# Overflow tables cut into parts behind the first expert gates, two low-part splits moved to GpSimd, and the order of four transfers changed, in an attention and mixture-of-experts layer on one core

## The chip, the cores and the metric

One core of one Trainium2 chip runs the whole program. Its engines run side by side and meet at semaphores: TensorE (PE, its weight loads PEld), VectorE (DVE), ScalarE (ACT), GpSimd (POOL), SyncE (SP, which here only issues transfers); 16 DMA engines carry the transfers. The metric is the device time of one execution, in microseconds (us), as the median of several runs.

## What is computed

The reference is one transformer layer on 1024 tokens of width 1024 in fp32: three kinds of attention, an output projection, and a hierarchical mixture of experts; then a last norm. The change lies in the experts, which compute

```python
for e in range(N_EXPERTS):                       # 32 experts, width 256
    a = hf @ w_e_gate[e]
    u = hf @ w_e_up[e]
    out = out + (jax.nn.silu(a) * u * gate[:, e:e + 1]) @ w_e_down[e]
```

where `gate` is zero for all but the two experts that the router chose for a token (top 2 of the 8 experts of the token's best group).

## The kernel before, in words

Each engine has its own program, written out by hand, and the order within a program is fixed. Attention, the output projection and the router (the norm, the logits, the choice of experts) come first. The experts are done as 34 tiles n = 0 to 33 of up to CAP = 96 tokens: one tile for each of the 32 experts and two for tokens that did not fit in their expert's 96 rows (overflow tiles, at n = 16 and n = 25). `TILE[n]` says which expert a tile belongs to.

One expert tile takes these steps. GpSimd gathers 96 token rows from the DRAM tensor `h2_d` into XG (`gather`, L916 before). TensorE transposes them (`x_transposes`, L2247, 8 products), ScalarE copies one half of the result to XT and VectorE the other (`m_x`), and TensorE multiplies with the gate and up matrices (`up_product`, L2256, 128 products). VectorE and ScalarE form the gated activation (`m_gate` on VectorE, `m_exp` on ScalarE) and cut it into a high part aTh and a low part aTl. The down matrix wdn is cut likewise: ScalarE writes the high part wdh (`m_split_hi`), VectorE the low part wdl (`m_split_lo`, L1802, two halves of 128x1024). TensorE multiplies them (`down_product`, L2266, 12 products), ScalarE and VectorE scale one half each into YO (`m_out`), and GpSimd adds the rows into `x2_d` (`scatter`, L928). On TensorE the order is up(n), transposes(n + 1), down(n - 1), up(n + 1) and so on.

The weights of a tile are 2 MB (wgu) and 1 MB (wdn). They go into a ring of RING = 6 slots; SyncE issues all of these transfers, in the order of its program, and one that waits holds up all behind it. The load of tile n (n >= 6) waits until down(n - 6) is done (the semaphore m_dn). The load of tile 5 goes where the overflow tables lie, so it waits for the last operation that uses them, `wrow_ov`.

The overflow tables are made by VectorE from the counts of the router (`overflow_tables`: in_tile, in_row, cj, ej, info), TensorE turns them into lists of token numbers (`overflow_ids` on TensorE, L2238, 16 products), and VectorE reads these (`overflow_ids` on VectorE: ids_ov, wo_hi, wrow_ov). Between the router and the first expert VectorE also works through a chain of small operations (s1 to s16, exc, eb, ge, geb, rae, rs, p1, sl, r, shf, shi, slo), all behind the count `v`; they end in shi and slo, from which only the overflow tables are made. `w_hi` and `wrow` are the weights of the tokens, first read when the output of tile 0 is scaled.

GpSimd's first gather waits for the token numbers `ids` of VectorE and for the stores of all token rows into `h2_d` (`h2_store`, semaphores h_st).

## Time and profile before

| | |
|---|---|
| median of 3 runs | 1179.07 us (1176.46 to 1182.43) |
| profiled execution, its own time | 1181.38 us |
| its span in the trace | 1179.6 us |
| TensorE busy | 1081.4 us, 92% |
| VectorE busy | 681.8 us, 58% |
| ScalarE busy | 448.4 us, 38% |
| GpSimd busy | 254.3 us, 22% |
| granted TensorE clock, mean | 0.972 of full speed |
| moved by DMA | 239.17 MB, mean 203 GB/s |

All times of one execution are counted from the start of its span. The 34 expert tiles take the stretch from about 811 us to 1151 us; what comes before is attention, projection and router, what comes after is the last norm. A share of busy time is an average over all of it and does not say what a stage waits for.

### The profile page before, as it was taken

The page shows a single profiled execution, that of the slowest core. Times are in us where ns is not written, and L with a number is a line of the kernel's source. Part 1 is how long each engine was busy: PE and PEld are TensorE (multiplying, and loading weights), DVE is VectorE, ACT ScalarE, POOL GpSimd, SP SyncE. Part 2 cuts the span into 40 slices and gives each one's busy share as a digit, 9 for nine tenths or more (in the row PEclk, how much of TensorE's full clock was granted, in tenths as well). Part 3 has the DMA queues.
Part 4 walks back from the last instruction along what each step waited for, and adds up shares of the span by engine and source line. Part 5 has one row for each costly group of instructions (what it writes and reads, how often), then busy time and mean ns, then how long its engine had stood idle before and what let it go on. Part 6 is the DMA issues. An engine that isn't in the chain of part 4 may idle for free.

```text
span 1179.6 us, 30191 instructions
## 1 busy us (share of the span) xinstructions
PE 1081.4 (92%) x12242; PEld 920.6 (78%) x12242; DVE 681.8 (58%) x1724; ACT 448.4 (38%) x761; POOL 254.3 (22%) x476
## 2 busy tenths in 40 slices
PE   5999899999999999999999899995989999989990
PEld 5989788778788888888877678885878887878770
DVE  4340445324666766665677533468767676767664
ACT  6321112221455555554576522221333343334323
POOL 1030000000332333321166300001223322222220
PEclk9999899999999999999999999995999999999995
DMA  9020855253656855565332255438899999999948
GB/s 362 21 89 2 291 178 161 107 161 141 156 120 149 207 148 119 120 140 131 107 83 57 104 214 202 138 119 315 309 370 366 362 354 350 344 360 356 354 142 298
DMA packets 62024, 239.17 MB, mean 203 GB/s; under 512 B 23328, under 2 KB 24128, under 8 KB 52032
## 3 DMA queue, kind: packets, MB, share of 16 engines
q1 hardware_dynamic: 54272, 220.45, 55.9%
q0 software_dynamic: 7616, 16.80, 6.1%
q8 instruction: 99, 1.62, 0.6%
q14 instruction: 37, 0.30, 0.1%
HBM read 201.14 MB, written 45.88 MB: 209 GB/s over the span
## 4 chain that ended last, share of the span: by engine, by line
PE 80%; DMA 6%; DVE 5%; issue 4%; ACT 2%; POOL 1%; SPq 1%; POOLq 0%; DVEq 0%; ACTq 0%
PE PS L2256 16%; PE PS L1920 13%; PE PS L2098 9%; PE PS L2266 8%; PE PS L2180 7%; PE PS L1909 6%; PE PS L2076 4%; PE PS L2037 4%; PE PS L2077 3%; PE PS L2247 2%; DMA wst<-in_wt 1%; DMA k<-T_d 1%; PE PS L1955 1%; PE PS L2070 1%; DMA h_d<-h 1%
## 5 line engine op out<-in xcount | busy, mean ns | idle before, releaser
L2256 PEld LDWEIGHTS PS<-XT,wgu 128*64 128x64 f32 x4352 | 185.8, 139 | 32.9 <-issue 32.9
L2256 PE MATMUL PS<-XT,wgu 128*64 128x96 f32 x4352 | 194.2, 250 | 18.0 <-issue 18.0
L1129 ACT ACTIVATE pt<-PS,cst 128x512 f32<-128x512 f32 (+3 forms) x288 | 167.2, 650 | 107.8 <-PE PS L2077 83.9
L1448 DVE CUSTOM_DVE_ANT_0 junkm<-PS,cst 128x512 f32<-128x512 f32 (+3 forms) x276 | 133.5, 531 | 78.4 <-PE PS L2037 76.3
L2098 PEld LDWEIGHTS PS<-V,pt 128*64 128x64 f32 x3840 | 121.6, 138 | 23.2 <-issue 12.0
L2098 PE MATMUL PS<-V,pt 128*64 128x65 f32 x3840 | 137.3, 225 | 0.9 <-issue 0.9
L1920 PE MATMUL PS<-hTh,wth 128*128 128x512 f32 x256 | 103.1, 403 | 5.1 <-DVE wtl L1295 5.1
L1920 PE MATMUL PS<-hTl,wth 128*128 128x512 f32 x256 | 100.7, 394 | 0.0
L1920 PE MATMUL PS<-hTh,wtl 128*128 128x512 f32 x256 | 100.7, 393 | 0.0
L843 POOL TENSOR_SCALAR_AFFINE_SELECT pt<-pt 128x128 f32<-128x128 f32 x224 | 64.1, 292 | 162.2 <-ACT pt L1129 119.1
L928 POOL DMA_INDIRECT x_d<-YO,ids x34 | 61.1, 1797 | 135.3 <-DVE YO L1811 100.9
L1802 DVE TENSOR_TENSOR wdl<-wdn,wdh 128x1024 fp32r<-128x1024 f32 x68 | 80.3, 1222 | 9.3 <-ACT wdh L970 9.2
L2037 PE MATMUL PS<-k,q 128*128 128x128 f32 (+3 forms) x324 | 79.5, 346 | 2.0 <-DMA k<-T_d 1.7
L2076 PE MATMUL PS<-q,k 128*128 128x512 f32 (+1 forms) x228 | 81.2, 370 | 0.0
L2077 PE MATMUL PS<-q,k 65*128 65x512 f32 (+1 forms) x240 | 76.4, 338 | 0.0
L970 ACT ACTIVATE wdh<-wdn 128x1024 fp32r<-128x1024 f32 x68 | 67.7, 1045 | 0.0
L1027 ACT ACTIVATE thi<-PS,cst 128x512 fp32r<-128x512 f32 x32 | 21.8, 686 | 113.7 <-PE PS L1920 92.3
L2037 PEld LDWEIGHTS PS<-k,q 128*128 128x128 f32 (+1 forms) x324 | 56.2, 190 | 10.6 <-DMA k<-T_d 2.5
L1193 ACT ACTIVATE ge<-ge 128x192 f32<-128x192 f32 x34 | 12.4, 364 | 136.8 <-DVE ge L1787 136.8
L1920 PEld LDWEIGHTS PS<-hTh,wth 128*128 128x128 f32 x256 | 48.7, 190 | 16.5 <-DVE wtl L1295 5.6
L916 POOL DMA_INDIRECT XG<-h_d,ids x34 | 33.7, 991 | 128.7 <-PE PS L2247 115.3
L1920 PEld LDWEIGHTS PS<-hTl,wth 128*128 128x128 f32 x256 | 48.8, 191 | 10.9 <-issue 1.0
(288 smaller groups left out, 1887.7 us busy)
## 6 DMA issues: line engine op xcount, KB each, us to landing
wgu<-in_wgu SPq DMA_DIRECT2D x34, 2048.0 KB, 17.6
wdn<-in_wdn SPq DMA_DIRECT2D x34, 1024.0 KB, 23.5
q<-T_d SPq DMA_DIRECT2D x58, 256.0 KB, 4.3
k<-T_d SPq DMA_DIRECT2D x58, 256.0 KB, 5.5
wst<-in_wt SPq DMA_DIRECT2D x16, 512.0 KB, 6.4
T_d<-thi SPq DMA_DIRECT2D x16, 512.0 KB, 2.6
T_d<-tlo SPq DMA_DIRECT2D x16, 512.0 KB, 3.9
xt<-in_x SPq DMA_DIRECT2D x8, 512.0 KB, 12.0
```

The costliest lines, as they stand in the source:

```text
L1129: ins = nc.scalar.activation(pt[:, (n + 2) % 6, 0:nt * P], PS[:, n % 3, 0:nt * P], ACT.Exp, scale=C("slopes", h, h + 1), bias=C("kb", w, w ...
L1448: V_.tensor_tensor_reduce(out=junk_[:, 0:L], in0=PS[:, bank, 0:L], in1=tab, scale=1.0, scalar=-3e38, op0=ALU.add, op1=ALU.max, accum_out=m ...
L1802: V_.tensor_tensor(out=wdl[n % RING][:, c, :], in0=wdn[n % RING][:, c, :], in1=wdh[n % 2][:, c, :].bitcast(f32), op=ALU.subtract).then_inc ...
L1909: ins = mm(o, x[:, k, t * P:(t + 1) * P], wv[w][:, k, :], start=(k == 0 and x is hTh and w == 0), stop=(k == KC - 1 and w == 1))
L1920: ins = mm(PS[:, 2 * p + h, :], w[:, p, k * P:(k + 1) * P], x[:, k, h * 512:(h + 1) * 512], start=(k == 0 and w is wth and x is hTh), stop ...
L2037: ins = mm(PS[:, bank, 0:nk * P], q_[:, t * P:(t + 1) * P], k_[:, k0 * P:(k0 + nk) * P], start=True, stop=True)
L2076: mm(o, k1[:, j * P:(j + 1) * P], q1[:, q], start=True, stop=False)
L2077: ins = mm(o, k2[0:HD + 1, j * P:(j + 1) * P], q2[0:HD + 1, q], start=False, stop=True)
L2098: ins = mm(PS[h * HD:(h + 1) * HD, O_BANK[b % 2], (t % 4) * VW:(t % 4 + 1) * VW], pt[0:rows, (n + 2) % 6, q * P + h * HD:q * P + (h + 1) * ...
L2180: ins = mm(PS[:, 2 + h, :], x[:, t % 2, k, :], w[:, k, h * 512:(h + 1) * 512], start=(k == 0 and x is oth and w is woh), stop=(k == KC - 1 ...
L2256: ins = mm(PS[h * HD:(h + 1) * HD, 2 + p, f * CAP:(f + 1) * CAP], wgu[q][:, c, lo:lo + HD], XT[:, p, c, :], start=(c == 0 and f == 0), sto ...
L2266: ins = mm(PS[0:CAP, 5 + h, :], x[:, p, c, :], w[:, c, cols], start=(c == 0 and x is aTh and w is wdh[p]), stop=(c == 1 and w is wdl[q]))
```

## The change

Lines marked - are taken out, lines marked + are put in; in between, only what the text speaks of is shown.

```diff
         # SyncE
                 if t + 1 == NT:
                     sp_.wait_ge(g_mm, 2 * NT)
-                    load_expert(TILE[2], 2)
+                    sp_.dma_start(wgu[2][:], a["wgu"][TILE[2]].rearrange("p (k n) -> p k n", k=KC)).then_inc(we_in[2], 16)
                 h2_store(t, p)
 
+            sp_.dma_start(wdn[2][:], a["wdn"][TILE[2]].rearrange("p (k n) -> p k n", k=2)).then_inc(we_in[2], 16)
             sp_.dma_start(wdn[3][:], a["wdn"][TILE[3]].rearrange("p (k n) -> p k n", k=2)).then_inc(we_in[3], 16)
...
             load_expert(TILE[4], 4)
+            sp_.wait_ge(m_dn, 1)
+            load_expert(TILE[RING], 0)
             sp_.wait_ge(dve_did, DV.of("wrow_ov"))
             load_expert(TILE[5], 5)
-            for n in range(RING, NB):
+            for n in range(RING + 1, NB):
         # GpSimd
+            def m_split_lo(n):
+                for c in range(2):
+                    pool.wait_ge(m_whi, 2 * n + c + 1)
+                    nc.gpsimd.tensor_tensor(out=wdl[n % RING][:, c, :], in0=wdn[n % RING][:, c, :],
+                                            in1=wdh[n % 2][:, c, :].bitcast(f32), op=ALU.subtract).then_inc(m_plo, 1)
             for n in range(NB):
                 gather(n)
+                if n in (2, 3):
+                    m_split_lo(n - 2)
         # VectorE
             red("v", vt[:, 0, 16:], cmp7[:], ALU.add)
+            m_x(0)
             src = 0
...
-            m_x(0)
-            overflow_tables()
-            m_split_lo(0)
             for n in range(NB):
                 m_gate(n)
                 if n == 0:
-                    overflow_ids()
+                    overflow_tiles()
                 if n:
                     m_out(n - 1)
-                if n + 1 < NB:
+                if n == 1:
+                    overflow_rows()
+                if n == 2:
+                    overflow_ids()
+                if 1 <= n < NB - 1:
                     m_split_lo(n + 1)
         # TensorE
             for n in range(NB):
                 m_up(n)
-                if n == 0:
-                    overflow_ids()
                 if n + 1 < NB:
                     m_transposes(n + 1)
+                if n == 2:
+                    overflow_ids()
                 if n:
                     m_down(n - 1)
```

`overflow_tables` is cut in two: `overflow_tiles` (the in_tile operations) stands behind the gate of tile 0, `overflow_rows` (in_row, cj, ej, info) behind the gate of tile 1 and the output of tile 0, and the reading of the lists behind the gate of tile 2 and the output of tile 1. The load of tile 5 still waits for `wrow_ov`. In `m_gate` of tile 0 the copy of XT for tile 1 stands ahead of the wait for ScalarE's exponential, no longer behind the reciprocal. The pair `w_hi`, `wrow` stands a few operations sooner. Some buffers lie elsewhere (ge, gd, aTh, aTl, and wdh of the odd tiles), and with it ScalarE's high split of tile 1 waits for the last x2 stores and not for TensorE's overflow product.

VectorE behind the chain of small operations that ends in slo, before (XT the transposed tokens, in_tile a table of tiles, wrow the weights of the tokens, cst the constants):

```order
L1736 SCALAR_TENSOR_TENSOR slo<-shi,slf 128x16 [waits dve_did]
L1740 COPY wrow<-PS 96x32 [waits pe_did,dve_did]
L1609 TENSOR_TENSOR wrow<-wrow,PS 96x32 [waits dve_did]
L1774 COPY XT<-PS 128x384 [waits m_tr,dve_did]
L1609 TENSOR_TENSOR in_tile<-shi,cst 128x8x22
L1609 TENSOR_TENSOR in_tile<-shi,cst 128x8x22 [waits dve_did]
```

And VectorE ahead of that chain now (the first row into vt is the count `v`):

```order
L1629 TENSOR_REDUCE vt<-cmp_153 128x32 [waits dve_did]
L1770 COPY XT<-PS 128x384 [waits m_tr,dve_did]
L1628 TENSOR_TENSOR vt<-vt 128x32
L1628 TENSOR_TENSOR vt<-vt 128x32 [waits dve_did] x4
L1629 TENSOR_REDUCE eb<-cmp_153 128x32 [waits dve_did]
L1628 TENSOR_TENSOR eb<-vt,eb 128x32 [waits dve_did]
```

The copy of tile 0's XT has moved from the end of the chain to its beginning, and the tables are gone from behind it.

VectorE at the end of the gate of tile 1, before (YO is the scaled output, here of tile 0; wdl with its numbers 195 is the low part for slot 2):

```order
L1796 CAST aTh<-gd 128x192 [waits link]
L1797 TENSOR_TENSOR aTl<-gd,aTh 128x192 [waits link]
L1811 TENSOR_SCALAR YO<-PS,wrow 96x512 [waits m_dn]
L1802 TENSOR_TENSOR wdl_195<-wdn_189,wdh_179 128x1024 [waits m_whi] x2
L1787 TENSOR_SCALAR ge<-PS 128x192 [waits m_gu]
```

And at the same place now (in_row, cj and ej are tables of rows and of tile numbers):

```order
L1794 CAST aTh<-gd 128x192 [waits link]
L1795 TENSOR_TENSOR aTl<-gd,aTh 128x192 [waits link]
L1809 TENSOR_SCALAR YO<-PS,wrow 96x512 [waits m_dn]
L1628 TENSOR_TENSOR in_row<-slo,cst 128x768
L1628 TENSOR_TENSOR in_row<-slo,cst 128x768 [waits dve_did]
L1628 TENSOR_TENSOR cj<-vt,cst 128x672 [waits dve_did]
L1629 TENSOR_REDUCE ej<-cj 128x21 [waits dve_did]
L1755 TENSOR_SCALAR ej<-ej 128x21 [waits dve_did]
L1757 TENSOR_SCALAR ej<-vt 128x1 [waits dve_did]
L1759 CAST info<-ej 1x22 [waits dve_did]
L1800 TENSOR_TENSOR wdl_195<-wdn_189,wdh_179 128x1024 [waits m_whi,dve_did]
L1800 TENSOR_TENSOR wdl_195<-wdn_189,wdh_179 128x1024 [waits m_whi]
```

Seven table operations have come in between the output of tile 0 and the low split of tile 2, and so ahead of the gate of tile 2, which is the next row into ge.

SyncE's weight transfers around the last token store, before (the number behind wgu and wdn goes with the slot: 183 and 189 are slot 2, 184 and 190 slot 3, 185 and 191 slot 4, 186 and 192 slot 5, 181 and 187 slot 0):

```order
L704 DMA wgu_183<-in_wgu 128x4096 [waits g_mm]
L705 DMA wdn_189<-in_wdn 128x2048
L718 DMA h_d<-h_142 128x1024 [waits h_xn]
L741 DMA wdn_190<-in_wdn 128x2048
L743 DMA wgu_184<-in_wgu 128x4096 [waits xg_in0]
L704 DMA wgu_185<-in_wgu 128x4096 [waits h_lg]
L705 DMA wdn_191<-in_wdn 128x2048
L704 DMA wgu_186<-in_wgu 128x4096 [waits dve_did]
L705 DMA wdn_192<-in_wdn 128x2048
L704 DMA wgu_181<-in_wgu 128x4096 [waits m_dn]
```

And now:

```order
L739 DMA wgu_183<-in_wgu 128x4096 [waits g_mm]
L719 DMA h_d<-h_142 128x1024 [waits h_xn]
L742 DMA wdn_189<-in_wdn 128x2048
L743 DMA wdn_190<-in_wdn 128x2048
L745 DMA wgu_184<-in_wgu 128x4096 [waits xg_in0]
L705 DMA wgu_185<-in_wgu 128x4096 [waits h_lg]
L706 DMA wdn_191<-in_wdn 128x2048
L705 DMA wgu_181<-in_wgu 128x4096 [waits m_dn]
L706 DMA wdn_187<-in_wdn 128x2048
L705 DMA wgu_186<-in_wgu 128x4096 [waits dve_did]
```

The last token store is one transfer further ahead, and the load of tile 6 (slot 0, behind down(0)) stands ahead of the load of tile 5 (slot 5, behind `wrow_ov`, which is the wait on dve_did).

On GpSimd the two halves of wdl of tile 0 stand between gather(2) and gather(3), those of tile 1 between gather(3) and gather(4); before, nothing but gathers and scatters stood there. On TensorE the 16 products of the overflow lists stand between the transposes of tile 3 and down(1), before between up(0) and the transposes of tile 1.

## Rows read from the trace of the kernel before

**Rows 1.** The page: DMA engines' busy tenths in 40 slices; GpSimd's queue: packets, MB, share.

```profile
DMA  9020855253656855565332255438899999999948
...
q0 software_dynamic: 7616, 16.80, 6.1%
```

**Rows 2.** Windows: length; busy us of PE, PEld, DVE, ACT, POOL; clock, DMA share, GB/s.

```profile
825.00:830.00 5.00, 2.57 (x33) 2.41 (x33) 4.39 (x11) 2.66 (x4) 0.96 (x1) 0.70 0.36 125
...
840.00:900.00 60.00, 57.05 (x950) 49.48 (x948) 42.85 (x68) 21.32 (x31) 19.22 (x13) 1.00 1.01 359
...
1135.00:1140.00 5.00, 5.00 (x98) 4.39 (x98) 4.64 (x9) 2.58 (x3) 1.45 (x1) 1.00 0.05 15
```

**Rows 3.** The chain that ended last: start us, us, what; up(2), up(32), up(33).

```profile
838.11 5.43 PE PS L2256 x128
...
1127.21 5.43 PE PS L2256 x128
...
1136.24 5.45 PE PS L2256 x128
```

**Rows 4.** SyncE's issues of loads 5, 8, 32; behind 8 and 32, their landing.

```profile
829.44 0.33 SPq L704 DMA_DIRECT2D wgu<-in_wgu  x1
...
856.55 0.43 SPq L705 DMA_DIRECT2D wdn<-in_wdn  x1
...
DMA to landing us min/median/max: 16.3/16.3/16.3
...
1088.51 0.43 SPq L705 DMA_DIRECT2D wdn<-in_wdn  x1
...
DMA to landing us min/median/max: 37.8/37.8/37.8
```

**Rows 5.** The chain around the first tiles: start us, us, what.

```profile
794.37 10.32 DMA h_d<-h
...
805.81 5.13 DMA XG<-h_d,ids
...
815.09 7.97 PE PS L2256 x128
...
827.67 6.83 PE PS L2256 x128
```

**Rows 6.** Timeline of the first tiles: start us, us, engine, line, op, tiles.

```profile
802.95 0.19 DVE L1699 TENSOR_SCALAR ids<-PS 96x32 uint32<-96x32 f32 x1 [0.24 <-PE PS L2215]
...
807.47 0.49 DVE L1610 TENSOR_REDUCE vt<-cmp 128x32 f32<-128x320 f32 x1
...
812.95 1.99 ACT L970 ACTIVATE wdh<-wdn 128x1024 fp32r<-128x1024 f32 x2
...
814.43 0.56 DVE L1774 COPY XT<-PS 128x384 f32<-128x384 f32 x1
...
814.91 0.70 DVE L1609 TENSOR_TENSOR in_tile<-shi,cst 128x176 fp32r<-128x176 f32 x2
...
817.91 1.95 DVE L1609 TENSOR_TENSOR in_row<-slo,cst 128x768 fp32r<-128x768 f32 x2
...
822.27 2.36 DVE L1802 TENSOR_TENSOR wdl<-wdn,wdh 128x1024 fp32r<-128x1024 f32 x2
...
834.54 0.36 DVE L1787 TENSOR_SCALAR ge<-PS 128x192 f32<-128x192 f32 x1 [2.73 <-PE PS L2256]
...
838.54 0.36 DVE L1797 TENSOR_TENSOR aTl<-gd,aTh 128x192 fp32r<-128x192 f32 x1
```

**Rows 7.** GpSimd's products of two SBUF tensors, and VectorE beside them.

```profile
59.88 7.32 POOL L805 TENSOR_TENSOR wnl<-wn,wnh 128x3296 fp32r<-128x3296 f32 x1 [33.58 <-ACT wnh L970]
...
60.78 7.50 DVE L1295 TENSOR_TENSOR wtl<-wst,wth 128x1024 fp32r<-128x1024 f32 x1 [9.42 <-ACT wth L970]
...
602.45 1.30 POOL L854 TENSOR_TENSOR wol<-wraw,woh 128x512 fp32r<-128x512 f32 x1
...
602.76 1.02 DVE L1518 TENSOR_SCALAR r<-r,nlam 128x4 f32<-128x4 f32 x1
```

More of the change, by code:

```diff
@@ L354, in program @@
         XT = at("XT", [P, 2, KC, CAP], f32, ZB + 56 * KB)
-        ge = at("ge", [P, 2 * CAP], f32, ZB + 24 * KB)
-        gd = at("gd", [P, 2 * CAP], f32, ZB + 25 * KB)
-        aTh = at("aTh", [P, 2, 2, CAP], f32r, ZB + 26 * KB)
-        aTl = at("aTl", [P, 2, 2, CAP], f32r, ZB + 26 * KB + 1536)
-        wdh = [at(f"wdh{p}", [P, 2, D], f32r, ZE + 24 * KB * p) for p in range(2)]
+        ge = at("ge", [P, 2 * CAP], f32, ZB + 62 * KB)
+        gd = at("gd", [P, 2 * CAP], f32, ZB + 62 * KB + 8 * CAP)
+        aTh = at("aTh", [P, 2, 2, CAP], f32r, ZE + 30 * KB)
+        aTl = at("aTl", [P, 2, 2, CAP], f32r, ZE + 30 * KB + 16 * CAP)
+        wdh = [at(f"wdh{p}", [P, 2, D], f32r, o) for p, o in enumerate((ZE, ZB + 24 * KB))]
         dead = (4 * COL["dist"][0] + 31) // 32 * 32
@@ L490, in program @@
         m_wlo = sem("m_wlo")
+        m_plo = sem("m_plo")
         m_dn = sem("m_dn")
@@ L550, in program @@
                     + [f"s{k}" for k in (1, 2, 4, 8, 16)]
-                    + ["exc", "eb", "ge", "geb", "rae", "rs", "p1", "sl", "r", "shf", "shi", "slo", "w_hi", "wrow",
+                    + ["exc", "eb", "ge", "geb", "rae", "rs", "p1", "w_hi", "wrow", "sl", "r", "shf", "shi", "slo",
                        "in_tile0", "in_tile1", "in_whi0", "in_wlo0", "in_tok0", "in_whi1", "in_wlo1", "in_tok1",
@@ L1208, in m_split_hi @@
                 act.wait_ge(we_in[n % RING], 32 * (n // RING + 1))
-                act.wait_ge(m_dn, n - 1) if n >= 2 else act.wait_ge(pe_did, PEV.of("ido" if n else "wrow"))
+                if n >= 2:
+                    act.wait_ge(m_dn, n - 1)
+                elif n == 1:
+                    for p in range(2):
+                        act.wait_ge(x2_st[p], 16 * NT // 2)
+                    act.wait_ge(h_xg, 2 * NT)
+                else:
+                    act.wait_ge(pe_did, PEV.of("wrow"))
                 for c in range(2):
@@ L1717, in _, with overflow_tiles @@
             red("v", vt[:, 0, 16:], cmp7[:], ALU.add)
[L1718 to L1743 removed]
+            def overflow_tiles():
                 eq = in_tile[:, :, :, 0, :]
@@ L1814, in _ @@
             m_x(0)
-            overflow_tables()
-            m_split_lo(0)
-            dve.wait_ge(h_ss, NT)
-            for p in range(2):
-                dve.wait_ge(x2_st[p], 16 * NT // 2)
+            src = 0
+            for k in (1, 2, 4, 8, 16):
+                tt(f"s{k}", vt[:, 1 - src, 16:], vt[:, src, 16:], vt[:, src, 16 - k:16 + NE - k], ALU.add)
+                src = 1 - src
+            inc = vt[:, src, 16:]
+            red("exc", eb[:], cmp7[:], ALU.add)
+            tt("eb", eb[:], inc, eb[:], ALU.subtract)
+            D_("ge", V_.tensor_scalar(out=rb[:], in0=rank, scalar1=float(CAP), scalar2=None, op0=ALU.is_ge))
+            D_("geb", V_.scalar_tensor_tensor(out=rc[:, 0, :], in0=eb[:], scalar=float(CAP), in1=C("e31"),
+                                              op0=ALU.mult, op1=ALU.add))
+            tt("rae", rb[:], rb[:], rc[:, 0, :].unsqueeze(1).broadcast_to([P, NT, NE]), ALU.mult)
+            tt("rs", ra[:], rank, C("ecap").unsqueeze(1).broadcast_to([P, NT, NE]), ALU.add)
+            tt("p1", ra[:], ra[:], rb[:], ALU.add)
+            dve.wait_ge(pe_did, PEV.of("wrow"))
+            D_("w_hi", V_.tensor_copy(out=wrow[0:CAP, 0:NE], in_=PS[0:CAP, 4, 64:64 + NE]))
+            tt("wrow", wrow[0:CAP, 0:NE], wrow[0:CAP, 0:NE], PS[0:CAP, 4, 64 + NE:64 + 2 * NE], ALU.add)
+            tt("sl", sel[:], ra[:].unsqueeze(1).broadcast_to([P, 2, NT, NE]), onehot[:], ALU.mult)
+            red("r", slf[:], sel[:], ALU.add)
+            D_("shf", V_.tensor_scalar(out=shi[:], in0=slf[:], scalar1=1.0 / CAP, scalar2=ROUND, op0=ALU.mult,
+                                       op1=ALU.add))
+            D_("shi", V_.tensor_scalar(out=shi[:], in0=shi[:], scalar1=-ROUND, scalar2=None, op0=ALU.add))
+            D_("slo", V_.scalar_tensor_tensor(out=slo[:], in0=shi[:], scalar=-float(CAP), in1=slf[:],
+                                              op0=ALU.mult, op1=ALU.add))
             for n in range(NB):
```

34 lines of the change are left out of this document (8 added, 26 removed).

## The prediction

> **What bounds the kernel now.** I read the slices of the page first. The DMA engines are half idle until the experts begin, and from there nearly full to the end of them [rows 1]. The windows of that stage say how full: share 1.01 at 359 GB/s over 840 to 900 us, while the stretch 835 to 1140 ends with a window of share 0.05, that is 0.25 us of work [rows 2]. So the last weights are in at about 1135.3. The chain that ended last runs through TensorE's products all the same: up(2) starts at 838.1, up(32) at 1127.2, up(33) at 1136.2 [rows 3]. The last two lie 9.0 apart, which is one tile on TensorE with no wait; the mean over the 30 tiles between up(2) and up(32) is 289.1 / 30 = 9.6, since TensorE also stands still now and then.
>
> Then the issues of the weight loads and their landings. The second half of load 8 is issued at 856.6 and lands 16.3 later, at 872.9; that of load 32 is issued at 1088.5 and lands 37.8 later, at 1126.3 [rows 4]. So 24 loads took 253.4 us, 10.6 each, against TensorE's 9.6: the queue gets later by one microsecond a tile. It began the stage far ahead and ends it level: load 32 lands 0.9 before up(32) starts, and the last transfer is done about 0.9 before up(33) starts. Before the stage the reader is to see a hole in the transfers, share 0.36 over 825 to 830 [rows 2]. From 829.4, when load 5 is issued [rows 4], they never stop. So two chains end this stage together: TensorE's, and the transfers', whose end moves with every microsecond that the engines idle once they could be loading. I count both.
>
> **The front of TensorE's chain.** The last token store takes 10.32 from 794.37, and the first gather starts at 805.81 [rows 5]. With 1 MB less ahead of it (2.8 us at 359 GB/s) the store lands near 801.9. The wait that then ends last is the one for the token numbers, ready at 803.1 [rows 6], 1.5 before the store's old landing at 804.7. So the gather moves forward by 1.5, and with it the rows of tile 0 (5.13 behind it [rows 5]) and load 3.
>
> VectorE now waits for tile 0's transposes right behind the count `v`, done at 807.96, and copies XT at 811.0 and not at 814.43 [rows 6]. Up(0) starts at 811.7, before 815.1, and is through in 7.97 (the clock is low there in both), at 819.6.
>
> The chain of small operations ran from 808.0 to the copy at 814.4 [rows 6], so 6.4 us. It now stands between this copy and the gate of tile 0: alone it would run from 811.6 to 818.0 and be hidden behind up(0). Here the moved splits come in. GpSimd took 1.30 for 128x512 and 7.32 for 128x3296 [rows 7]; by the line through both, 128x1024 takes 2.4, a tile's two halves 4.8 (VectorE's two took 2.36 [rows 6]). They start when ScalarE's first high half is done (1.0 each [rows 6], from 811.5), so they cover 812.8 to 817.8.
>
> What does VectorE do beside them? Beside the longer of them its subtraction of two SBUF tensors, which otherwise takes 1.2 us, took 7.50 from 60.78 and ended 1.1 behind GpSimd's product of 59.88 to 67.20 [rows 7]. A 128x4 operation from 602.76 took 1.02 and ended level with GpSimd's of 602.45 to 603.75. VectorE stood still until GpSimd was done. This bears on nearly all of the chain: eb, geb, rae, p1, wrow, sl and slo read two tensors of SBUF, and only a few read PSUM. So each half holds VectorE for about 2 of its 2.4 us; one operation slips in between. The chain ends at 821.9 and the gate of tile 0 starts 2.3 late, not on time.
>
> The Trainium skill, page "SBUF — State Buffer", section "SBUF: two separate sides", says the same: the port pair that VectorE and GpSimd share is locked for a whole instruction, against VectorE operations with two SBUF inputs and those in a two-port mode. It speaks against this change, and the two pairs of rows agree with it; by it the sum is the one worked out here, without it rival 1.
>
> From there: the gate's first operation, then XT of tile 1 on both engines at 823.2, and up(1) at 823.3, before 827.67 [rows 5]: 4.4 ahead. Its 6.83 contain a fall of the granted clock (mean 0.70 over 825 to 830 [rows 2]) behind a wait of TensorE of 2.4; I leave 2.8 of wait there, and so keep 6.83: up(1) ends at 830.1. The splits of tile 1 run on GpSimd from 824.3 to 829.3 and hold up the last two operations of gate 0 (aTh, aTl) until 829.7; down(0), which comes behind up(1) and the transposes, does not wait for it.
>
> The tiles part of the tables took 814.91 to 817.9, so 3.0, the rows part 817.91 to 822.2, so 4.3 [rows 6]. A gate takes 3.0 from its first operation to the end of the XT copy, 4.4 to aTl (834.54 to 838.9 [rows 6]). Behind gate 0 the tiles part ends at 832.75, 2.6 after up(1); XT of tile 2 is there at 835.7, and up(2) starts at 835.8, 2.2 ahead of before. Behind gate 1 (837.1) come the output of tile 0 (0.8), the rows part (4.3) and the low split of tile 2 (2.4): gate 2 begins at 844.7, though up(2) ended at 841.2. XT of tile 3 is ready at 847.7, and up(3) starts at 847.8, before 847.1. TensorE's 1.5 for the overflow products lie inside this wait. Then gate 2, the output of tile 1 and the reading of the lists: `wrow_ov` is done at 850.5. From tile 4 on VectorE is on time again. TensorE's chain alone therefore comes out 0.7 late: what the front gains (3.4, then 4.4) the parts and the lock take back.
>
> **The transfers.** Load 5 waits for `wrow_ov`: issue at 850.6, before 829.4 [rows 4], 21 later. Load 6 takes its place, but can't go before down(0) ends at 833.8. Its 3.1 MB need 8.8 at 359 GB/s and about 1 to begin: done at 843.6. Then SyncE waits, with loads 5 and 7 both behind the same wait, and the engines stand idle but for a gather and a scatter until 851.6. Before, load 5 was through by the same reckoning at 839.2 (829.4 + 1 + 8.8), and from there 28 loads ran on without a gap. The same number (5 and 7 to 33) now starts at 851.6: 12.4 later. One gather and one scatter fewer stand in their way: GpSimd's queue moved 16.8 MB [rows 1] in 68 transfers, so 0.5 MB, 1.4 us. So the last landing moves by 11.0, and of this 0.9 was free: up(33) starts 10.1 later. Load 5 itself lands near 861, up(5) wants it at 866; nothing stalls there, the bill comes at the end, when TensorE's waits for weights set in around tile 22. I take 9 of the 10.1, since the lock's overlap (2 us a half) is the softest term and can only be less.
>
> **What costs nothing, and why.** ScalarE's high split of tile 1 waits for stores long done. The wdn part of load 2 lands 1.3 later, some 20 before its use. GpSimd's gather(3) and gather(4) stand behind splits that end 2.7 and 1.7 before their transposes free them; without this cover a gather would be late by the difference. `w_hi` and `wrow` are early in either place.
>
> **Rivals.** (1) The lock bites little: VectorE's small operations get in first, and GpSimd waits. Against it stand the two pairs of [rows 7], for it that they are only two. Then up(1) starts at 821.6, the clock may hold, up(2) starts at 830.8, load 5 is issued at 845.3, the 28 loads start 7.1 later, less 1.4 and 0.9: +5, 1184.
>
> (2) The transfers give way: faster with fuller queues, or the engines' end not tied to the last landing. Then TensorE's chain counts, with the lock: +0.7, 1180. Against it: 359 GB/s at share 1.01 with two loads queued as with four. The Trainium skill, "HBM Reference", section "Specifications (TRN2)", gives about 425 GB/s for a core that streams alone; by it a load with its gather and scatter would take 8.9 and not 10.6, and this rival would hold. The trace disagrees for this mix.
>
> (3) Faster: rivals 1 and 2 at once, in one mechanism, that the stage is TensorE's alone and VectorE's parts fit behind its products. Up(4) then starts 4.5 earlier, up to 6 if the clock does not fall at up(1): 1174. It decides if load 33 lands more than 5 us ahead of its use after a 12 us later start, which 0.9 of slack speaks against.
>
> (4) Worse: the clock falls a second time in the waits ahead of up(2) and up(3) (2.0 and 1.4 long), and `wrow_ov` slips by 1.5 to 5: +11 to +14, 1192.
>
> **The numbers.** The profiled execution took 1181.38 (span 1179.6), 2.3 over the median of 1179.07. The sum is a difference against that span, and I put it on the median: 1179.07 + 9 = 1188. Chances: forecast 0.46, rival 1 0.22, rival 2 0.12, rival 3 0.13, rival 4 0.07. The forecast's own range is 1185 to 1191. The range leaves out rival 3 and most of rival 4: 1178 to 1192. Half a per cent is 5.9 us, about what a measurement of this kernel can tell from no change (its three runs lie 6 apart). Faster: half of rival 3, 0.07. Slower: nine tenths of the forecast (0.41), a third of rival 1 (0.07), all of rival 4: 0.55. The rest, 0.38, within.
>
> **What would show it.** Up(0) near 811.7 and up(1) near 823; VectorE operations of 2 us where 0.2 was the rule, each ending with a GpSimd subtraction; up(3) near 848; load 5 issued near 850 with a hole of some 8 us ahead of it; waits of TensorE for weights from about tile 22 on, and a last landing near 1146. The forecast is wrong if load 5 is issued before 842, or if the last ten tiles still follow each other 9.0 us apart.

## The result, and the profile after

The changed kernel takes 1185.54 us (median of 20 runs, 1180.21 to 1192.85), the kernel before 1180.99 (20 runs, 1176.46 to 1184.1). The ratio is 1.0037, with a 95% interval of 1.0024 to 1.005: 4.5 us slower, which lies inside half a per cent. One execution of each kernel was profiled, 1183.62 after and 1181.38 before, so the two traces show 2.2 of the 4.5 us.

The page after: busy time of the engines, and the DMA engines' busy tenths in 40 slices.

```profile
PE 1081.6 (92%) x12242; PEld 921.3 (78%) x12242; DVE 683.5 (58%) x1720; ACT 448.6 (38%) x761; POOL 264.1 (22%) x480
...
DMA  9020855253655855565332355438699999999958
```

TensorE did the same work. In the row of the transfers three digits moved by one, and one by more: slice 29 fell from 8 to 6 [rows 1]. From there on the slices are as full as before, so what is missed there has to be made up later or comes on top.

The windows, with the columns of [rows 2] (the last three: granted clock, DMA share, GB/s):

```profile
825.00:830.00 5.00, 5.00 (x98) 4.89 (x94) 4.86 (x6) 0.00 (x0) 3.60 (x2) 0.79 0.06 19
830.00:835.00 5.00, 3.82 (x25) 2.66 (x25) 4.33 (x10) 2.02 (x4) 0.97 (x1) 1.00 0.38 89
...
845.00:850.00 5.00, 3.84 (x87) 3.54 (x87) 4.76 (x11) 2.58 (x3) 0.75 (x1) 1.00 0.37 108
...
820.00:855.00 35.00, 30.03 (x463) 26.49 (x462) 31.59 (x58) 10.13 (x16) 12.54 (x8) 0.95 0.65 223
```

There are two holes, one ahead of load 6 and one ahead of load 5. Over 820 to 855 the DMA engines moved 0.223 x 35 = 7.8 MB. The same window of the kernel before reads

```profile
820.00:855.00 35.00, 32.57 (x534) 29.24 (x532) 26.43 (x45) 10.44 (x16) 7.58 (x6) 0.95 0.89 323
```

which is 11.3 MB. The third busy time is VectorE's: 31.6 of 35 us after, 26.4 before, and TensorE (the first) gives up 2.5 us.

The timeline after, which answers to [rows 6] and to SyncE's issues in [rows 4]; in brackets the idle time before a row and its releaser:

```profile
812.35 4.68 POOL L940 TENSOR_TENSOR wdl<-wdn,wdh 128x1024 fp32r<-128x1024 f32 x2
812.83 4.26 DVE L1628 TENSOR_TENSOR eb<-vt,eb 128x32 f32<-128x32 f32 x1
817.12 0.42 DVE L1820 TENSOR_SCALAR rb<-PS 128x256 f32<-128x256 f32 x1
...
821.75 0.36 DVE L1783 TENSOR_SCALAR ge<-PS 128x192 f32<-128x192 f32 x1
...
822.93 7.15 PE L2279 MATMUL PS<-XT,wgu 128*64 128x96 f32 x128 [2.63 <-ACT XT L982]
823.91 4.68 POOL L940 TENSOR_TENSOR wdl<-wdn,wdh 128x1024 fp32r<-128x1024 f32 x2 [1.86 <-ACT wdh L982]
824.99 1.39 DVE L1794 CAST aTh<-gd 128x192 fp32r<-128x192 f32 x1
826.42 2.40 DVE L1795 TENSOR_TENSOR aTl<-gd,aTh 128x192 fp32r<-128x192 f32 x1
...
833.72 0.33 SPq L705 DMA_DIRECT2D wgu<-in_wgu  x1
...
836.68 1.99 DVE L1628 TENSOR_TENSOR in_row<-slo,cst 128x768 fp32r<-128x768 f32 x2
...
841.09 2.36 DVE L1800 TENSOR_TENSOR wdl<-wdn,wdh 128x1024 fp32r<-128x1024 f32 x2
843.37 0.35 DVE L1783 TENSOR_SCALAR ge<-PS 128x192 f32<-128x192 f32 x1
...
848.72 0.17 DVE L1628 TENSOR_TENSOR wrow<-wrow,PS 96x21 f32<-96x21 f32 x1
848.91 0.33 SPq L705 DMA_DIRECT2D wgu<-in_wgu  x1
```

First see the 128x32 operation into eb. It took 4.26 us and ended at 817.09, level with GpSimd's pair (812.35 + 4.68 = 817.03). Then aTh and aTl of tile 0: 1.39 and 2.40, where 0.36 was usual for aTl [rows 6]. GpSimd's second pair runs from 823.91 to 828.59 in two halves of 2.3; aTh ends at 826.4, 0.1 after the first half, and aTl at 828.8, 0.2 after the second. So gate 0 starts at 821.75, load 6 at 833.72, and `wrow_ov`, with load 5 right behind it, is done at 848.9.

The chain that ended last, after, beside [rows 3]:

```profile
834.87 5.50 PE PS L2279 x128
...
846.49 5.50 PE PS L2279 x128
...
1052.31 37.73 DMA wdn<-in_wdn
...
1090.17 4.80 PE PS L2279 x111
...
1138.67 5.46 PE PS L2279 x128
```

Up(2) stands 3.2 earlier than before, up(33) 2.4 later. Between them the chain now runs through a load: a down matrix issued at 1052.3 lands at 1090.0 and releases up(28). It is TensorE's only wait for weights over 860 to 1178 us:

```profile
PE PS L2279 <- DMA wdn<-in_wdn: 1.2, 1, 1.2
```

This is where the time is lost. Up(27) still starts level with the kernel before, and up(28) 2.1 later. Before:

```profile
1078.85 5.43 PE PS L2256 x128
...
1088.10 4.76 PE PS L2256 x111
```

After:

```profile
1078.91 5.65 PE L2279 MATMUL PS<-XT,wgu 128*64 128x96 f32 x128
...
1090.17 4.80 PE L2279 MATMUL PS<-XT,wgu 128*64 128x96 f32 x111 [1.19 <-DMA wdn<-in_wdn]
```

Last, the landings of loads 8, 32 and 33 after (SyncE's second issue of each; [rows 4] has 8 and 32 of before):

```profile
L706 SPq DMA_DIRECT2D wdn<-in_wdn x1: 447/447/447, 856.0 to 856.0; - x1
DMA to landing us min/median/max: 24.3/24.3/24.3
...
L706 SPq DMA_DIRECT2D wdn<-in_wdn x1: 428/428/428, 1089.4 to 1089.4; - x1
DMA to landing us min/median/max: 39.3/39.3/39.3
...
L706 SPq DMA_DIRECT2D wdn<-in_wdn x1: 472/472/472, 1101.2 to 1101.2; - x1
DMA to landing us min/median/max: 35.9/35.9/35.9
```

Load 8 lands at 880.3 (872.9 before), load 32 at 1128.7 (1126.3 before), load 33 at 1137.1, 1.6 ahead of up(33). So 7.4 us of delay at load 8 were 2.4 at load 32: the 24 loads between took 248.4 us and not 253.4. TensorE has 10 to 13 other waits, of up to 2.5 us, behind up(4) in each trace, 12 to 16 us in all, for which the profile shows no releaser; what they are stays open.

### The profile page after: what moved, and what is told of

Same layout as the page of the kernel before. It is cut to its first block, busy times and chain, and to the rows that moved or that the text cites. A ratio compares the mean times of both kernels' runs of the same rounds, so it can differ in the third digit from the quotient of the medians.

```text
span 1181.6 us, 30191 instructions
## 1 busy us (share of the span) xinstructions
PE 1081.6 (92%) x12242; PEld 921.3 (78%) x12242; DVE 683.5 (58%) x1720; ACT 448.6 (38%) x761; POOL 264.1 (22%) x480
## 4 chain that ended last, share of the span: by engine, by line
PE 76%; DMA 9%; DVE 6%; issue 4%; ACT 2%; SPq 1%; POOL 1%; DVEq 0%; POOLq 0%; ACTq 0%
PE PS L2279 14%; PE PS L1943 13%; PE PS L2121 9%; PE PS L2203 7%; PE PS L2289 7%; PE PS L1932 6%; PE PS L2099 4%; PE PS L2060 4%; PE PS L2100 3%; DMA wdn<-in_wdn 3%; PE PS L2270 2%; DMA wst<-in_wt 1%; DMA k<-T_d 1%; PE PS L1978 1%; DMA wn<-in_wn 1%
## 5 line engine op out<-in xcount | busy, mean ns | idle before, releaser
L1800 DVE TENSOR_TENSOR wdl<-wdn,wdh 128x1024 fp32r<-128x1024 f32 x64 | 75.6, 1222 | 9.8 <-ACT wdh L982 9.7
L1205 ACT ACTIVATE ge<-ge 128x192 f32<-128x192 f32 x34 | 12.4, 363 | 141.6 <-DVE ge L1783 141.6
L1320 DVE SCALAR_TENSOR_TENSOR tlo<-PS,cst,thi 128x512 fp32r<-128x512 f32 x32 | 23.5, 748 | 58.3 <-ACT thi L1039 58.1
## 6 DMA issues: line engine op xcount, KB each, us to landing
xt<-in_x SPq DMA_DIRECT2D x8, 512.0 KB, 12.1
```

The source lines that it names most:

```text
L1800: V_.tensor_tensor(out=wdl[n % RING][:, c, :], in0=wdn[n % RING][:, c, :], in1=wdh[n % 2][:, c, :].bitcast(f32), op=ALU.subtract).then_inc ...
```

## The experiments

Two theories were to be told apart. **Theory T**: the stage ends with the stream of weights, so its delay (load 6 behind down(0), load 5 behind `wrow_ov`) is what costs. **Theory V**: VectorE is the full engine, so what it is given or what holds it (the table parts, the lock by GpSimd) delays TensorE's front, and that costs. Theory F in one text is V's end: only TensorE's front decides. Each kernel was timed beside the kernel before.

For reading across them, one table. All but the first column is from each kernel's one trace, counted from the start of the operation that makes the token numbers `ids` (it stands at 796.8 to 804.3 in the runs, so the stages ahead differ by some us). "Landing 8" is the landing of the second half of load 8, "change" the ratio minus one, times 1180.99, in us.

| kernel | change | up(1) | up(4) | load 6, load 5 issued | landing 8 | landing 33 | up(33) |
|---|---|---|---|---|---|---|---|
| before | 0 | 24.7 | 53.1 | 35.2, 26.5 | 69.9 | 332.3 | 333.3 |
| the change | +4.4 | 19.9 | 52.5 | 30.7, 45.9 | 77.2 | 334.0 | 335.6 |
| load 6 first in before | +7.7 | 24.8 | 54.5 | 36.6, 37.4 | 78.5 | 337.7 | 339.7 |
| load 5 behind the product | +3.1 | 20.4 | 54.4 | 31.0, 40.0 | 74.2 | 333.0 | 334.9 |
| no split on GpSimd | -0.1 | 18.0 | 47.6 | 27.1, 41.0 | 72.9 | 328.6 | 330.6 |
| load 5 sooner in before | 0.0 | 24.7 | 54.4 | 36.5, 21.2 | 70.5 | 331.8 | 333.7 |
| readiness order | -5.1 | 18.6 | 49.6 | 31.2, 20.4 | 65.0 | 325.8 | 327.5 |
| load 5 in two parts | +2.2 | 19.5 | 53.8 | 30.3, 39.1 | 69.4 | 330.2 | 333.8 |
| store sooner alone | -0.5 | 24.7 | 53.1 | 35.2, 26.5 | 70.8 | 331.3 | 334.2 |
| splits back on VectorE | +3.7 | 17.7 | 53.4 | 26.8, 45.8 | 77.0 | 335.7 | 338.5 |
| readiness order, load 6 first | -2.4 | 18.6 | 49.9 | 31.1, 32.0 | 72.6 | 331.1 | 332.9 |

(The landing of load 33 before is the prediction's 1135.3, read from a window's share. It is some tenths too late: from 1134.5 on that trace moves only 0.05 MB on the queue of the loads, so the weights were in by about 1134.8.) In every trace the last landing stands 1 to 3.6 ahead of up(33): the two chains stay together to the end, whichever of them was made late.

Where they come together can be read from the traces. By the starts of the up products behind `ids`, the distance to the kernel before changes in net by 1.4 us at most from up(6) to up(26). Between up(26) and up(29) it grows by 2.9, 4.0, 2.9, 3.6, 2.9, 7.0 and 3.0 us in the changed kernel and in experiments 1, 2, 3, 6, 8 and 9, and by 0.3, 1.2 and 0.1 in experiments 4, 5 and 7. The first seven are the traces in which TensorE waits for weights, 1.2 to 3.6 us in all; the others have 0.2 or none. Only in experiment 6 does this happen with a stream that is not late, behind a front that is 4.2 ahead at up(26).

One thing more differs between these kernels, and neither theory has it: the granted clock. Within the runs of the kernel before (three sets of 17 to 35) the time falls by 0.9 to 1.0 us for each 0.001 of mean granted clock. Experiment 1 ran at 0.9678 on average and the kernel before beside it at 0.9697, experiment 3 at 0.9719 against 0.9697, experiment 5 at 0.9725 against 0.9700, experiment 8 at 0.9718 against 0.9700, experiment 9 at 0.9728 against 0.9688; the rest differ by 0.0011 at most. With 0.95 us for 0.001 taken out, the changes of experiments 1 to 9 would be +5.9, +4.2, +2.0, +0.3, -2.7, +2.3, -0.2, +5.5 and +1.3, an estimate. These follow landing 8 more closely than the medians do. How much of the clock the edits bring about, through shorter or longer waits of TensorE, and how much is chance, no run separates. The traces are single executions too: that of experiment 3 is the fastest of its twelve (1175.02, at 0.976), that of experiment 8 is 2.6 above its median.

### 1. Load 6 first, in the kernel before

```diff
             load_expert(TILE[4], 4)
+            sp_.wait_ge(m_dn, 1)
+            load_expert(TILE[RING], 0)
             sp_.wait_ge(dve_did, DV.of("wrow_ov"))
             load_expert(TILE[5], 5)
-            for n in range(RING, NB):
+            for n in range(RING + 1, NB):
```

> The kernel before with one edit on SyncE: the load of tile 6 is issued ahead of the load of tile 5, as in the change. TensorE, VectorE and ScalarE are untouched. Theory T (the end of the stage moves with the start of the unbroken stream of weight loads): load 5 goes out at about 838.6 instead of 829.4, the transfer engines stand idle for some 9 us, and the stream begins 9 later. In the changed kernel a start about 9 later gave +4.5 by the medians, so +3 to +6 here too, ratio 1.003 to 1.005, with TensorE's first products where they were. Theory F (the end moves with TensorE's front alone): load 5 still lands before its use at 865, so ratio 1.000, within 0.1%.

1189.53 us, ratio 1.0065 (1.0042 to 1.0088). VectorE and TensorE have their old programs, and up(1) stands where it stood. The transfers stop, as the windows of this kernel show (the third, later one is for the clock):

```profile
830.00:835.00 5.00, 5.00 (x72) 5.00 (x70) 3.16 (x6) 0.00 (x0) 0.00 (x0) 0.54 0.01 3
835.00:840.00 5.00, 5.00 (x73) 4.25 (x69) 2.19 (x4) 0.85 (x2) 0.96 (x1) 1.00 0.00 0
...
875.00:880.00 5.00, 4.81 (x47) 4.37 (x47) 1.47 (x3) 0.85 (x2) 0.00 (x0) 0.66 1.01 368
```

and TensorE's waits over 860 to 1178 us (us in total, times, longest) have an entry for weights, which the kernel before has not:

```profile
PE PS L2258 <- DMA wdn<-in_wdn: 2.0, 2, 1.5
```

Load 5 waits 11 us longer behind another load's wait, load 8 lands 8.6 later, and the end comes 7.7 later. A late stream makes the kernel slower: T holds, and the cost is above the range expected.

Not all of the 7.7 is the stream's. The clock of 0.54 over 830 to 835 was 0.95 before:

```profile
830.00:835.00 5.00, 5.00 (x110) 4.88 (x108) 2.17 (x3) 0.07 (x1) 0.00 (x0) 0.95 0.93 338
```

It makes up(2) 1.4 later, ahead of anything that load 5 could hold up. Behind a wait of 2.2 the clock falls again (0.66 over 875 to 880), and up(6) is 3.0 later. Up(26) is 2.5 later, and only from there to up(29) does it become 6.5, with the waits for weights.

### 2. Load 5 behind the overflow product, in the changed kernel

```diff
-            sp_.wait_ge(dve_did, DV.of("wrow_ov"))
+            sp_.wait_ge(pe_did, PEV.of("ido"))
+            sp_.wait_ge(dve_did, DV.of("info"))
             load_expert(TILE[5], 5)
```

> The changed kernel with one edit on SyncE: load 5 waits for TensorE's overflow products (842.5 in the changed kernel) and for the last table operation of VectorE (841.1), not for the reading of the lists (848.9). Theory T: load 5 is issued at about 842.6, while load 6 still runs; the hole of 6 us in the transfers is gone, the last landing comes 5 to 6 sooner, and the time falls back to where TensorE's chain ends: ratio to before 0.998 to 1.000. Theory F: nothing moves, ratio stays at 1.004.

1183.94 us, ratio 1.0026 (1.0005 to 1.0047): a miss, most of the loss is still there. The issue came 5.9 sooner and load 8 landed 3.0 sooner, but the first hole (825 to 835, ahead of load 6) stayed, and load 5 still waits behind both parts of the tables. T predicts a gain of the size of the landing's, 3 us; the medians give 1.3, and the intervals overlap, so this run tells little of T.

### 3. Without the splits on GpSimd

This kernel leaves out the low part of the down matrices of tiles 0 and 1: ScalarE writes a plain copy of the matrix in its place, and GpSimd does nothing between its gathers.

```diff
             for n in range(NB):
                 gather(n)
-                if n in (2, 3):
-                    m_split_lo(n - 2)
...
+                if n < 2:
+                    act.wait_ge(m_whi, 2 * n + 2)
+                    for c in range(2):
+                        copy(wdl[n % RING][:, c, :], wdn[n % RING][:, c, :]).then_inc(m_plo, 1)
```

> The changed kernel without the two splits on GpSimd: the low part of the down matrices of tiles 0 and 1 is not computed; ScalarE writes a plain copy there (1 us per half, where it is idle). Theory L (GpSimd's products of two SBUF tensors hold VectorE's): the operation that took 4.26 us takes 0.2, the chain of small operations ends at about 817.8, the first gate is on time, up(1) starts near 820.5, up(2) near 830, load 5 is issued near 845, and with it the end moves 2 to 4 sooner than in the changed kernel: ratio to before 1.000 to 1.002. Rival: the 4.26 us were VectorE waiting for something else (a semaphore, its own queue); then they stay, and up(1) stays at 822.9.

1180.45 us, ratio 0.9999 (0.9985 to 1.0013). Its timeline:

```profile
806.54 0.19 DVE L1624 TENSOR_TENSOR eb<-vt,eb 128x32 f32<-128x32 f32 x1
...
813.32 0.36 DVE L1779 TENSOR_SCALAR ge<-PS 128x192 f32<-128x192 f32 x1 [2.02 <-PE PS L2275]
...
816.99 0.26 DVE L1790 CAST aTh<-gd 128x192 fp32r<-128x192 f32 x1
817.28 0.36 DVE L1791 TENSOR_TENSOR aTl<-gd,aTh 128x192 fp32r<-128x192 f32 x1
```

The same operations take 0.19, 0.26 and 0.36 once GpSimd is idle: the three were held for 4.1 + 1.1 + 2.0 = 7.2 us. VectorE is ready 2.0 before the gate of tile 0 could start, and everything behind it comes sooner. By the medians the whole loss of the change is gone with the two pairs; by the estimate for the clock, 2.0 of it would be left. In this trace the clock did not fall at up(1), so up(4) at 47.6 is better than the edit alone makes it.

### 4. Load 5 sooner, in the kernel before

The edit of experiment 2, made in the kernel before, where it takes away the hole at 825 to 830.

> The kernel before with one edit on SyncE: load 5 waits for TensorE's overflow products and the last table operation, not for the reading of the lists: issue at about 824.6 instead of 829.4, which closes the hole in the transfers over 825 to 830. TensorE's chain is untouched. Theory T with slack: TensorE's chain ends the stage in the kernel before, the transfers land 4 to 5 sooner and give nothing or little: ratio 0.998 to 1.000. If the transfers alone bound the kernel before: 0.996 to 0.997.

1180.49 us, ratio 1.0000 (0.9984 to 1.0016). The hole did not go, it moved, as the windows of this kernel show (share 0.36 and 0.98 before):

```profile
825.00:830.00 5.00, 2.58 (x32) 2.61 (x34) 4.65 (x11) 2.31 (x4) 0.96 (x1) 0.60 0.93 359
...
835.00:840.00 5.00, 5.00 (x56) 3.77 (x53) 3.82 (x9) 1.68 (x4) 0.96 (x1) 1.00 0.19 56
```

The transfers finish load 5 sooner and then wait for down(0), which frees the slot for load 6 no sooner than before (in this trace 1.3 later, since the clock stayed low longer: 0.71 over 830 to 835, 0.95 before). Load 8 lands at 70.5, not sooner than the 69.9 of before. An idle stretch counts only if the work behind it could have started.

### 5. An order by readiness

From the kernel before: token store sooner, as in the change; VectorE copies XT of tile 0 within the chain and that of tile 1 within the tables; TensorE transposes tile 1 ahead of the overflow products; the low split of tile 0 stands behind gate 0, those of tiles 1 and 2 behind gate 1; load 5 waits as in experiment 2 and goes ahead of load 6. The tables stay before gate 0, and GpSimd splits nothing. The core of the diff:

```diff
-            sp_.wait_ge(dve_did, DV.of("wrow_ov"))
+            sp_.wait_ge(pe_did, PEV.of("ido"))
+            sp_.wait_ge(dve_did, DV.of("info"))
...
-            m_x(0)
             overflow_tables()
-            m_split_lo(0)
...
                 if n == 0:
+                    m_split_lo(0)
                     overflow_ids()
                 if n:
                     m_out(n - 1)
-                if n + 1 < NB:
+                if n == 1:
+                    m_split_lo(1)
+                if 1 <= n < NB - 1:
                     m_split_lo(n + 1)
...
                 m_up(n)
-                if n == 0:
-                    overflow_ids()
                 if n + 1 < NB:
                     m_transposes(n + 1)
+                if n == 0:
+                    overflow_ids()
```

> Made from the kernel before, with nothing on GpSimd: the token store one transfer sooner, the XT copies of tiles 0 and 1 on VectorE set into the chain where their inputs are ready, ScalarE's XT copy of tile 1 ahead of its exponential, the transposes of tile 1 ahead of the overflow products on TensorE, the low splits of tiles 0 and 1 behind their gates, and load 5 behind the overflow products and the last table operation. The tables stay ahead of the first gate. Theory V+T (VectorE's work is the limit of the front, and the transfers' unbroken stream begins with load 6 at the end of down(0)): up(0) near 811.7, up(1) near 822 to 823 as in the changed kernel, but gates 1 and 2 on time, up(2) near 833 (838.1 before), load 6 issued near 832.7 (838.1) with load 5 already running; both chains 4 to 5 ahead: ratio to before 0.996 to 0.997. Rival: the transfers' rate alone decides and gives no more than the 0.9 of slack: 0.999 to 1.000.

1174.71 us, ratio 0.9957 (0.9938 to 0.9975): faster than both kernels, and a little more than expected. Its windows have no hole:

```profile
810.00:820.00 10.00, 10.00 (x180) 9.84 (x178) 8.73 (x23) 0.49 (x1) 1.48 (x1) 0.85 1.01 397
820.00:830.00 10.00, 8.31 (x105) 6.76 (x100) 8.76 (x18) 3.00 (x5) 1.63 (x1) 0.83 0.97 358
830.00:840.00 10.00, 10.00 (x162) 8.37 (x163) 9.31 (x15) 3.85 (x6) 5.99 (x2) 1.00 0.91 330
```

Up(1) comes 6.1 sooner, load 8 lands 4.9 sooner, the end comes 5.1 sooner. Both chains are moved here, so this run does not tell T from V. The tables cost TensorE nothing where they lie behind up(0), whose products take 8 us at the low clock.

### 6. Load 5 in two parts

In the changed kernel, the down matrix of load 5 goes ahead of load 6 (it waits for `slo` and for TensorE's reading of the weights `wrow`), and the rest behind load 6 waits as in experiment 2.

```diff
             load_expert(TILE[4], 4)
+            sp_.wait_ge(dve_did, DV.of("slo"))
+            sp_.wait_ge(pe_did, PEV.of("wrow"))
+            sp_.dma_start(wdn[5][:], a["wdn"][TILE[5]].rearrange("p (k n) -> p k n", k=2)).then_inc(we_in[5], 16)
             sp_.wait_ge(m_dn, 1)
             load_expert(TILE[RING], 0)
```

> The changed kernel with load 5 cut in two on SyncE: its 1 MB part as soon as VectorE's chain of small operations is done (821.7), its 2 MB part behind the overflow products and the last table operation (842.5). Theory T: the transfers fill 3 us of the hole over 826 to 835 and all of the one over 844 to 850, the stream is 9 us ahead of the changed kernel's at load 7, and the ratio to before falls from 1.004 to 1.000, within 0.15%. If the changed kernel's loss sits in TensorE's front (its three waits of 2.6, 1.2 and 1.2): 1.003 to 1.004 as before.

1182.95 us, ratio 1.0019 (0.9994 to 1.0043): inconclusive. Load 8 lands at 69.4, as early as before, and still the median is 2.2 above; the interval holds both nothing and all of the 4.4. If the 2.2 are real, the stream's start alone does not explain them. In the trace up(29) is 1.3 ahead of the kernel before; then the clock falls once more behind a wait of 2.3, and up(30) is 0.5 late.

### 7. The token store sooner, alone

```diff
-                    load_expert(TILE[2], 2)
+                    sp_.dma_start(wgu[2][:], a["wgu"][TILE[2]].rearrange("p (k n) -> p k n", k=KC)).then_inc(we_in[2], 16)
                 h2_store(t, p)
 
+            sp_.dma_start(wdn[2][:], a["wdn"][TILE[2]].rearrange("p (k n) -> p k n", k=2)).then_inc(we_in[2], 16)
```

> The kernel before with the token store alone moved one transfer sooner. Theory V (VectorE is busy without a gap from 806 to the first gate, so it sets up(1)): the gather starts 1.5 sooner, up(0) does not (VectorE copies XT at 814.4 as before), up(1) and all behind it stay: ratio 1.000, within 0.1%. Rival (my own term, 1.5 of the front's gain from the store): 0.9987.

1179.69 us, ratio 0.9996 (0.9972 to 1.0019). Up(0) to up(4) stand where they stood, at 12.1, 24.7, 35.1, 44.1 and 53.1. An earlier gather is of no use while VectorE copies XT only at the end of its chain: VectorE sets the front. The ratio's interval holds the rival's 0.9987 as well; the trace tells them apart.

### 8. The splits back on VectorE

The changed kernel with the low splits of tiles 0 and 1 behind gate 0 on VectorE, around the tiles part.

```diff
-                if n in (2, 3):
-                    m_split_lo(n - 2)
...
                 if n == 0:
+                    m_split_lo(0)
                     overflow_tiles()
+                    m_split_lo(1)
```

> The changed kernel with the low splits of tiles 0 and 1 back on VectorE, around the tiles part of the tables: that of tile 0 behind gate 0, that of tile 1 ahead of the output of tile 0. The lock of some 7 us is gone, 4.8 us of VectorE's own work come back. Theory L: VectorE saves 2 us up to up(3): up(1) near 820.5, up(2) near 834, load 5 issued 1 to 3 sooner than 848.9, ratio to before 1.002 to 1.003. Rival: VectorE's work is worth the same wherever it stands, ratio 1.004.

1183.45 us, ratio 1.0031 (1.0016 to 1.0046). The lock is gone and the time is not, by the medians. Load 6 is issued 3.9 sooner than in the changed kernel, but load 5, with load 7 and all others behind it, at the same 45.8 behind `ids`, and load 8 lands at the same 77.0. T names the reason. The work put behind gate 0 also cost TensorE: its chain has

```profile
831.83 8.33 PE PS L2273 x128
```

and its windows

```profile
825.00:830.00 5.00, 2.40 (x11) 1.38 (x9) 4.40 (x9) 0.91 (x3) 1.06 (x1) 1.00 0.54 140
830.00:835.00 5.00, 3.17 (x40) 3.21 (x42) 4.83 (x9) 2.29 (x3) 0.36 (x1) 0.59 0.95 401
```

Up(2) took 8.33 and not 5.50. TensorE had stood still for 4.4 us ahead of it (2.60 of the first window, and 830 to 831.83), and over 830 to 835 the granted clock was 0.59, so mostly at the lower of the two levels, 1.2 of 2.4 GHz.

### 9. The readiness order with load 6 first

The edit of experiment 1, made in the kernel of experiment 5 (load 5 keeps that kernel's waits).

> The readiness order (the run before of that name: ratio 0.996) with one thing swapped: load 6 is issued ahead of load 5, so load 5 waits behind it on SyncE until down(0) has ended. TensorE's front should stand as in that run: up(1) some 18.6 us and up(2) some 31 us behind the ids record. Load 6 issued about 30.5, load 5 about 31.5 behind the ids record, so the DMA engines should stand near idle for some 8 us before them. Theory T (the start of the stream of weights decides): the end comes 5 to 8 us later than in the readiness order, ratio to the kernel before 1.000 to 1.003. Theory F (TensorE's front of the stage decides, the transfers have slack): ratio stays at 0.995 to 0.997.

1179.31 us, ratio 0.9980 (0.9965 to 0.9996), between the two expectations. TensorE's front is that of experiment 5 within 0.3 us (up(1) to up(4) at 18.6, 31.1, 40.1 and 49.9), so Theory F's 0.995 to 0.997 asked for no loss. Landing 8 is 7.6 later, and the trace's up(33) 5.4 later; the ratios give 2.7 us, and their intervals just overlap. Of the 5.4, 3.0 are there at up(12), behind a wait of 2.5 with a clock of 0.81 and 0.84 over 920 to 930 (1.00 in experiment 5), and 1.8 come at up(28), where TensorE waits 1.3 for weights. Against the kernel before, load 8 lands 2.7 later and the kernel is 2.4 faster, which T alone does not allow; but by the estimate for the clock it would be 1.3 slower, which T does allow. So Theory F is refuted, and that the front counts beside the stream is not shown by this run.

## Why the prediction was right, and where it was not

The range held the time, and the direction was that of the forecast. The size was half: +4.5 against +9, so the case that came true is "within half a per cent", which had 0.38. That 1185.54 is only 2.5 from the 1188 is partly luck: the sum stood on a median of 1179.07 from three runs, and twenty give 1180.99. Step by step:

**The front of TensorE's chain: right to 1.4 us.** Forecast up(0) 811.7, gate 0 821.9, up(1) 823.3, up(2) 835.8, gate 2 844.7, up(3) 847.8; measured 811.35, 821.75, 822.93, 834.87, 843.37, 846.49. So the chain is 0.6 ahead at up(3) where the sum had it 0.7 late.

**The lock: right.** GpSimd's pair took 4.68 (4.8 forecast). That nothing slips in between the halves of the first was more than forecast: one 128x32 operation was held through both. In the second pair aTh did get in, as forecast. Experiment 3 takes the pairs out and shows the same operations at 0.19 to 0.36. The Trainium skill, "SBUF — State Buffer", section "SBUF: two separate sides", says that a GpSimd instruction holds the shared port pair for its whole length; the trace agrees, for operations with two SBUF inputs and for the CAST into aTh, while two operations that read PSUM took their usual 0.35 at 824.22 and 824.60, beside the first half of GpSimd's second pair. 4.68 us of GpSimd twice cost VectorE 7.2, where it does one such pair itself in 2.36 [rows 6]. Rival 1 gave 1184, nearest to the measured time, but its mechanism (small operations get in first) did not occur; the number is near for another reason, below.

**The issue of load 5: right.** 848.9 against 850.6, load 6 at 833.7 against 833.8, and the hole is there. Experiment 1 shows that such a hole costs by itself (+7.7, an estimated 5.9 without the clock), experiment 9 that it costs in a better order too (2.7, an estimated 4.0).

**The term that was mis-sized: "12.4 later".** It set the stream's start in the kernel before at 839.2 and after at 851.6. By landings, load 8 came only 7.4 later. At the prediction's own 10.6 a load it should have landed three loads behind these points, at 870.9 and 883.3; it landed at 872.9 and 880.3. So of the 5.0 between, 2.0 lie in the reckoning of 839.2, which had the stream before too early, 1.7 are the earlier issue of load 5, and for the last 1.3 the three loads from load 5 on ran faster (the sum's 1.4 for a gather and a scatter is of this kind and was taken off elsewhere).

**The term that was missing: the stream makes up time.** The sum let every microsecond of delay at the start stand at the end, less 1.4 for a gather and a scatter. Measured, the 24 loads from 9 to 32 took 248.4 instead of 253.4. In experiments 1, 2, 3, 8 and 9, whose load 8 landed late, they took 250.9, 250.5, 247.4, 250.1 and 250.1; in the kernels with load 8 near 70 or sooner (experiments 4 to 7) 252.9, 252.6, 252.2 and 251.9. Against the 253.4 of before the regained time is 2.5 to 6 us, and not the same for equal delays. Why is open in part. Between the two landings the windows read, for the changed kernel

```profile
880.30:1128.70 248.40, 233.80 (x3774) 200.87 (x3770) 172.85 (x280) 86.82 (x127) 70.81 (x51) 1.00 1.02 361
```

and for the one before

```profile
872.90:1126.30 253.40, 242.23 (x3894) 207.65 (x3890) 178.81 (x290) 90.00 (x132) 72.57 (x52) 1.00 1.02 356
```

so the share is the same and the rate is not. The queues of these two stretches, loads and then gathers with scatters (packets, MB, share), read for the changed kernel

```profile
q1 hardware_dynamic: 7007, 76.50, 80.1%
q0 software_dynamic: 5693, 12.58, 20.9%
```

and for the one before

```profile
q1 hardware_dynamic: 7040, 76.71, 79.8%
q0 software_dynamic: 5820, 12.90, 21.2%
```

Since TensorE is late, fewer gathers and scatters stand among the same loads: 51.9 us of the engines' time and not 53.7. That is 1.8 of the 5. The loads themselves took 199.0 and not 202.2, and only 0.6 of this is for fewer bytes; 2.6 us are a better rate, 2.60 and not 2.64 us a MB. Why is open. No run changed the mix alone.

**"From this 0.9 was free": wrong in kind.** The landing of load 33, at 1137.1 and not near 1146, is still 1.6 ahead of up(33), and before it was about 1.4 ahead. The waits for weights did not set in at tile 22 and go on: there is one, of 1.2 us at up(28), where the chain falls back by 2.1. So the last tiles do follow each other 9.0 apart from up(30) on, which the prediction had named as a sign against itself for all of the last ten.

**The maximum of two chains: too simple.** I took the later of TensorE's +0.7 and the stream's +9. The stream meets TensorE at up(27) to up(29), and what it takes there is less than its delay at the start. With TensorE's program held, 8.6 us at landing 8 cost 7.7 (experiment 1) and 7.6 us cost 2.7 (experiment 9), by the estimate without the clock 5.9 and 4.0; with a front 5.5 sooner at up(4), a landing 3.0 later cost nothing by the medians and 2.0 by that estimate (experiment 3). A part for the front beside the stream is possible, and not shown. Rival 2 (the transfers give way altogether) is refuted by experiments 1 and 9, rival 3 with it. Rival 4's second fall of the clock did not come in the changed kernel (1.00 over 830 to 835), but does exist: experiment 8 has it.

Experiments 3 and 8 together say what the splits on GpSimd cost: 4.5 us against not doing them, of which about 1 goes with the clock, and against doing them on VectorE no difference that these intervals tell, since load 5 waits for the same `wrow_ov` in either. The table parts behind the gates are argued to be another part, which no run took out alone: VectorE was busy 4.65 of 5 us at 845 to 850 even before, so 7 us of tables there push the next gates, while ahead of gate 0 they lay behind up(0). How the 4.5 us divide exactly is not settled.

## What to carry to other kernels

In a queue that issues in order, a transfer that waits holds all behind it: put it behind the waits that end sooner, and look at what the engines could load meanwhile, not at the hole alone. Work that was moved to GpSimd, with two SBUF inputs, was not off VectorE here; measure how long VectorE's small operations beside it become. Where two chains end a stage together, a delay of one need not be paid in full, so price it by an experiment that delays that one alone, find the tile at which it is paid, and compare the granted clocks before reading a difference of a few microseconds.
